# A 2-block transformer kernel on one Trainium2 core: narrow projections with their weight columns stationary, a reordered pool layer, and an output product that runs with tokens on the partitions

## The reference

```
# first block, mixer: proj = xn @ w_in; its last 80 columns are k_idx (64) and w_idx (16)
logits = einsum('bthd,bsd->bths', q_idx, k_idx)
idx_score = einsum('bth,bths->bts', w_idx * (IDX_HEADS**-0.5 * IDX_DIM**-0.5), relu(logits))
# pool layer: u, zu (1536 each), qm, zm (512 each) = split(rmsnorm(x) @ w_in)
y_pool = (windowed means of u, minus u) @ w_pool * scale * silu(zu)
y_mem = memory_attention(qm / sqrt(128), mem) * silu(zm)
x = x + concat([y_pool, y_mem]) @ w_out
# NSA layer: q (1536), gl (36), zq (1536), qm, zm (512 each) = split(rmsnorm(x) @ w_in)
gates = sigmoid(gl)                  # 12 heads x 3 branches
x = x + concat([nsa(q, gates, ...) * silu(zq), y_mem * silu(zm)]) @ w_out
return rmsnorm(x, final_g)
```

## Time and profile before

| | |
|---|---|
| median of 3 runs | 2564.04 us |
| profiled execution, its own time | 2564.2 us |
| its span, first to last instruction | 2562.5 us |
| mean granted TensorE clock | 0.965 |
| PE, PE weight load, POOL, ACT, DVE busy | 94%, 88%, 80%, 41%, 37% |

### The profile page before, as it was taken

The page is one execution under the profiler, slowest core; times in us unless marked ns, Lnnn a source line. Parts: engine busy times, 40 slices in busy tenths (PEclk is TensorE's granted clock), DMA queues, the critical chain, the costliest instruction groups (busy, mean ns, idle before and its releaser), DMA issues. The chain is left out here.

```text
span 2562.5 us, 43002 instructions
## 1 busy us (share of the span) xinstructions
PE 2406.2 (94%) x17211; PEld 2267.3 (88%) x17211; DVE 951.0 (37%) x1451; ACT 1044.7 (41%) x1308; POOL 2060.7 (80%) x1940
## 2 busy tenths in 40 slices
PE   6999999989998899999999999998899998999896
PEld 6989998768997798898998999998899888988896
DVE  5025662554152442031121131704516652255522
ACT  3344444554345333333333333434334333345532
POOL 6988994766786599999999998799787986865583
PEclk9999998999998899999999999999899998999998
DMA  5654433353443355655555555455354564533341
GB/s 183 197 165 148 147 121 120 116 197 116 165 148 116 115 166 196 196 174 194 191 180 197 182 180 177 156 184 161 120 181 148 165 191 153 163 107 116 100 164 50
DMA packets 206428, 400.17 MB, mean 156 GB/s; under 512 B 10434, under 2 KB 20932, under 8 KB 205252
## 3 DMA queue, kind: packets, MB, share of 16 engines
q1 hardware_dynamic: 206276, 397.99, 47.9%
HBM read 395.87 MB, written 2.10 MB: 155 GB/s over the span
## 5 line engine op out<-in xcount | busy, mean ns | idle before, releaser
L566 POOL TENSOR_TENSOR w_low<-ring,w_high 128x512 fp32r<-128x512 f32 (+3 forms) x1872 | 2050.9, 1128 | 457.7 <-ACT w_high L1091 450.1
L1091 ACT ACTIVATE w_high<-ring 128x1024 fp32r<-128x1024 f32 (+2 forms) x760 | 786.6, 1039 | 1364.0 <-PE bank L599 1351.3
L599 PE MATMUL bank<-x_high,w_high 128*128 128x256 f32 x4196 | 1220.3, 291 | 77.6 <-issue 32.6
L599 PE MATMUL bank<-x_low,w_high 128*128 128x256 f32 x4196 | 1203.8, 287 | 0.0
L599 PE MATMUL bank<-x_high,w_low 128*128 128x256 f32 x4196 | 1203.3, 287 | 0.0
L599 PEld LDWEIGHTS bank<-x_high,w_high 128*128 128x128 f32 x4196 | 822.7, 196 | 94.0 <-issue 50.0
L599 PEld LDWEIGHTS bank<-x_low,w_high 128*128 128x128 f32 x4196 | 823.0, 196 | 2.2 <-issue 2.0
L599 PEld LDWEIGHTS bank<-x_high,w_low 128*128 128x128 f32 x4196 | 822.1, 196 | 0.0
L599 PE MATMUL bank<-w_high,hidden 128*128 128x512 f32 x768 | 236.5, 389 | 0.0
L599 PEld LDWEIGHTS bank<-w_high,hidden 128*128 128x128 f32 x768 | 144.0, 188 | 29.7
L599 PE MATMUL bank<-w_high,x_high 128*128 128x512 f32 (+2 forms) x352 | 142.5, 405 | 9.0 <-DVE proj L1581 5.9
(11 more groups left out here) (272 smaller groups left out, 1961.5 us busy)
## 6 DMA issues: line engine op xcount, KB each, us to landing
ring<-in_w_in SPq DMA_DIRECT2D x64, 1024.0 KB, 5.4
ring<-in_w_up SPq DMA_DIRECT2D x64, 1024.0 KB, 5.2
ring<-in_w_down SPq DMA_DIRECT2D x64, 1024.0 KB, 5.1
ring<-in_w_out SPq DMA_DIRECT2D x48, 1024.0 KB, 5.1
ring<-in_a_w_in SPq DMA_DIRECT2D x32, 1024.0 KB, 5.3
ring<-in_b_w_in SPq DMA_DIRECT2D x32, 1024.0 KB, 5.3
ring<-in_w_kv SPq DMA_DIRECT2D x24, 1024.0 KB, 5.1
ring<-in_w_mem_kv SPq DMA_DIRECT2D x16, 1024.0 KB, 5.0
```

Source lines behind the costliest of these rows:

```text
L566: last = pool.tensor_tensor(w_low[:, u % UNITS, part], ring[:, u // 2, first:first + n], w_high[:, u % UNITS, part], ALU.subtract)
L599: mm = pe.matmul(out, lhs, rhs, start=start and n == 0, stop=stop and n == 2, skip_group_check=True)
L1091: act.activation(w_high[:, u % UNITS, 0:n], ring[:, u // 2, r0 * g.width:r0 * g.width + n], ACT.Copy)\
```

## The change

It has five parts. (a) `idx_tail` and `nsa_gate` use a new `narrow_unit`: the 80 or 36 weight columns are stationary and the 256 tokens move, 6 matmuls a unit in place of 12. The index keys then come out with features on the partitions and go straight to `ikT`; the 16 index weights and the 36 gates are turned by two transposes each (`idx_turned`, `turn_gates`). (b) The pool layer runs `pool_qm`, `pool_zm`, `pool_in`; the first 16 units of `pool_in` run beside the 4 memory heads, the windowed means are computed while later blocks of `pool_in` run, and `out0` takes its operand's last quarter first (`GATED_FIRST`). (c) ACT rounds 9 units in place of 6 before it waits for `turn_hidden`. (d) `out1` runs in `tokens_unit`; the residual `hT` is turned into `tokens` by 8 groups of 4 transposes between the units of `nsa_q` (`turn_h`), with a copy by ACT each. (e) The last norm runs on the token rows, block by block: DVE adds, multiplies by the gain (loaded as a broadcast of 1 MB), ACT squares with accumulation, then one root a row, a scaling shared by DVE and ACT, and a store in four pieces.

```diff
-     ("pool_in", 6, 6), ("pool_qm", 1, 1), ("pool_zm", 1, 1), ("pool_mix", 1, 4, 3, 384), ("out0", 4, 4),
+     ("pool_qm", 1, 1), ("pool_zm", 1, 1), ("pool_in", 6, 6), ("pool_mix", 1, 4, 3, 384), ("out0", 4, 4),
...
+        GATED_FIRST = (3, 0, 1, 2)
+        BESIDE_MEM0 = units_of("pool_in")[:16]
...
+        H_TURN_AFTER = (11, 13, 14, 16, 18, 20, 21, 22)
...
-        TOKENS_FIRST = ("attn_v", "cross_v", "mem_v0", "mem_v1", "nsa_gate")
+        TOKENS_FIRST = ("attn_v", "cross_v", "mem_v0", "mem_v1")
...
-        peel = g.blocks if g.blocks < 3 else int(g.b0 == 0)
+        peel = g.blocks if g.blocks < 3 or name == "out0" else int(g.b0 == 0)
...
+    out0_part = columns(w_out2[0:D, :], 0)
+    stream("out0", lambda n, j: out0_part(n, GATED_FIRST[j]))
...
+    sp.wait_ge(h_turned, 8)
+    sp.wait_ge(x_ready, x_made["nsa"] + 4)
+    sp.dma_start(final_gain, spread(a["final_g_2"].rearrange("(o n) -> o n", o=1), 0, P)).then_inc(final_gain_in, 16)
...
-    sp.wait_ge(final_kept, 8)
-    sp.dma_start(a["out"].rearrange("a (h p) n -> p (a h) n", p=P), tokens).then_inc(out_stored, 16)
...
+    out_rows = a["out"].rearrange("a (h p) n -> p (a h) n", p=P)
+    for piece in range(2):
+        for h in range(TH):
+            cols = slice(1024 * piece, 1024 * piece + 1024)
+            sp.wait_ge(final_rows[h], piece + 1)
+            sp.dma_start(out_rows[:, h, cols], tokens[:, h, cols]).then_inc(out_stored, 16)
+    sp.wait_ge(out_stored, 64)
...
+    def narrow_unit(g, b, u, pair, x, first, of):
+        pe.wait_ge(low_ready, 8 * b + u + 1)
+        wh, wl = parts(u, g)
+        r0, rows = g.unit(u)
+        for k in range(rows):
+            kt = first + r0 + k
+            mm = accumulate(pair[0][0:g.width, 0:T], (wh[:, k, :], wl[:, k, :]), x(kt),
+                            start=(kt == 0), stop=(kt == of - 1))
+        mm.then_inc(units_used, 1)
...
-            pe.wait_ge(idx_keys, 1)
+            pe.wait_ge(evacuated, PLAN["idx_tail"].g0 + 1)
             for h in range(TH):
-                mm = pe.transpose(bank[4][0:64, h * P:h * P + P], idx_rows[:, h, 0:64], ident[:, :])
+                mm = pe.transpose(bank[4][:, 16 * h:16 * h + 16], idx_w_rows[:, h * P:h * P + P],
+                                  ident[64:80, 64:80])
             mm.then_inc(idx_turned, 1)
         if n == 6:
-            pe.wait_ge(idx_keys, 2)
+            pe.wait_ge(idx_keys, 1)
+            pe.wait_ge(idx_weights, 1)
...
-    product("pool_in", features_unit, operand, made=x_made["pool"], sums=norm_sum)
-    product("pool_qm", features_unit, operand)
+    product("pool_qm", features_unit, operand, made=x_made["pool"], sums=norm_sum)
+    product("pool_zm", features_unit, operand)
     pe.wait_ge(evacuated, PLAN["pool_zm"].g0)
-    attend(MEM0, units_of("pool_zm"))
+    attend(MEM0, BESIDE_MEM0)
+    product("pool_in", features_unit, operand, begun=2)
...
+    product("out0", features_unit, lambda kt: operand(4 * GATED_FIRST[kt // 4] + kt % 4), made=x_made["pool_y"])
...
+        for h in range(TH):
+            mm = pe.transpose(bank[4][:, 36 * h:36 * h + 36], gate_rows[:, h * P:h * P + P], ident[0:36, 0:36])
+        mm.then_inc(gates_turned, 1)
...
+        pe.wait_ge(evacuated, PLAN["out0"].g0 + 4)
+        pe.wait_ge(silu_ready, 5)
+        if i:
+            pe.wait_ge(h_kept, i)
+        for k in range(4):
+            mm = pe.transpose(bank[4][:, k * P:k * P + P], hT[:, 4 * (i // 2) + k, (i % 2) * P:(i % 2) * P + P],
+                              ident[:, :])
+        mm.then_inc(h_turned, 1)
...
+    beside = {9: turn_hidden, 10: turn_gates, 12: second_layer, 15: swap_compressed}
...
+        if n in H_TURN_AFTER:
+            turn_h(H_TURN_AFTER.index(n))
...
-    product("out1", features_unit, operand, made=x_made["nsa_y"])
-    norm_sum()
...
-        if n >= 2:
-            pe.wait_ge(final_kept, n - 1)
-        h, c = n % 2, n // 2
-        for k in range(4):
-            mm = pe.transpose(bank[5 + n % 2][:, k * P:k * P + P], proj[:, 4 * c + k, h * P:h * P + P],
-                              ident[:, :])
-        mm.then_inc(final_turned, 1)
+    product("out1", tokens_unit, operand, made=x_made["nsa_y"])
...
+    high_parts("pool_qm", root)
+    high_parts("pool_zm")
+    attend(MEM0, BESIDE_MEM0)
+    def silu_of(t, group):
+        act.wait_ge(evacuated, group + 1)
         act.activation(pair_tile(t, 4), pair_tile(t, 4), ACT.Silu).then_inc(silu_ready, 1)
-    high_parts("pool_qm")
-    attend(MEM0, units_of("pool_zm"))
-    act.wait_ge(evacuated, PLAN["pool_mix"].g0)
-    act.activation(pair_tile(28, 4), pair_tile(28, 4), ACT.Silu).then_inc(silu_ready, 1)
+    silu_of(28, PLAN["pool_zm"].g0)
+    high(20)
+    silu_of(12, PLAN["pool_in"].g0 + 3)
+    high(8)
+    silu_of(16, PLAN["pool_in"].g0 + 4)
+    high(4)
+    silu_of(20, PLAN["pool_in"].g0 + 5)
...
-    high(6)
+    high(9)
...
+    high(1)
+    act.wait_ge(gates_turned, 1)
+    act.activation(nsa_gates[:, :, :].rearrange("p h n -> p (h n)"), bank[4][:, 0:36 * TH], ACT.Sigmoid)\
+       .then_inc(silu_ready, 1)
+    done = 14
+    for i, n in enumerate(H_TURN_AFTER):
+        high(n + 5 - done)
+        done = n + 5
+        act.wait_ge(h_turned, i + 1)
+        act.activation(tokens[:, i % 2, (i // 2) * 512:(i // 2) * 512 + 512], bank[4][:, :], ACT.Copy)\
+           .then_inc(h_kept, 1)
+    high(36 - done)
...
+    for j in range(4):
+        high(8)
+        act.wait_ge(evacuated, PLAN["out1"].g0 + j + 1)
...
+            act.activation(final_spare, tokens[:, h, 512 * j:512 * j + 512], ACT.Square,
+                           accum_out=final_sums[:, h, j:j + 1]).then_inc(final_squares, 1)
+    act.wait_ge(final_squares, 4 * TH)
+    act.activation(final_spare[:, 0:1], eps_col[:, 0:1], ACT.Sqrt)
+    act.wait_ge(final_summed, 1)
+    act.activation(final_dev, final_mean, ACT.Sqrt, scale=1.0 / D, bias=eps_col[:, 0:1]).then_inc(final_sqrt, 1)
+    act.wait_ge(final_root, 1)
+    act.activation(tokens[:, 1, 0:1024], tokens[:, 1, 0:1024], ACT.Copy, scale=final_scale[:, 1:2])\
+       .then_inc(final_rows[1], 1)
+    act.activation(tokens[:, 1, 1024:1536], tokens[:, 1, 1024:1536], ACT.Copy, scale=final_scale[:, 1:2])
+    act.activation(tokens[:, 1, 1536:D], final_last[:, 1, :], ACT.Copy, scale=final_scale[:, 1:2])\
+       .then_inc(final_rows[1], 1)
...
-    pair = bank[2 * (g.g0 % 2)], bank[2 * (g.g0 % 2) + 1]
-    for h in range(TH):
-        last = dve.tensor_scalar(idx_rows[:, h, 0:64], pair[h][:, 0:64], scale_col(h), None, ALU.mult)
...
+    tail = bank[2 * (g.g0 % 2)]
+    then(dve.tensor_tensor(ikT[0:64, :], tail[0:64, 0:T], scale_rows_[0:64, :], ALU.mult))
+    dve.tensor_copy(ikT[64:128, :], ikT[0:64, :]).then_inc(idx_keys, 1)
+    dve.scalar_tensor_tensor(out=idx_w_rows, in0=tail[64:80, 0:T], scalar=IDX_SCALE, in1=scale_rows_[64:80, :],
+                             op0=ALU.mult, op1=ALU.mult).then_inc(evacuated, 1)
...
-            dve.tensor_copy(ikT[64:128, :], bank[4][0:64, 0:T]).then_inc(idx_keys, 1)
+            dve.tensor_copy(idx_w[:, :, :].rearrange("p h n -> p (h n)"), bank[4][:, 0:16 * TH])\
+               .then_inc(idx_weights, 1)
+            dve.wait_ge(idx_weights, 1)
...
+    keep("pool_qm", scaled_tiles(24))
+    keep("pool_zm", scaled_tiles(28))
+    attend(MEM0, BESIDE_MEM0, {"pool_in": scaled_tiles(0)})
...
+    def pool_block(b):
+        read_out(PLAN["pool_in"], b, 0, scaled_tiles(0))
+        dve.wait_ge(evacuated, PLAN["pool_in"].g0 + b + 1)
+    pool_block(2)
+    dve.wait_ge(silu_ready, 1)
+    then(dve.tensor_tensor(pair_tile(24, 4), pair_tile(24, 4), pair_tile(28, 4), ALU.mult))
+    window(3)
+    pool_block(3)
+    window(2)
+    window(0)
+    pool_block(4)
+    window(1)
+    for n in range(4):
+        dve.wait_ge(units_used, behind("pool_in")((3 * n + 2) // 2))
+        split(pair_tile(32 + 3 * n, 3), flat(x_high, 3 * n, 3), flat(x_low, 3 * n, 3)).then_inc(x_ready, 1)
+    pool_block(5)
+    split(pair_tile(24, 4), flat(x_high, 12, 4), flat(x_low, 12, 4)).then_inc(x_ready, 1)
+    def pooled_y(c):
+        split(pair_tile(12 + 4 * c, 4), flat(x_high, 4 * c, 4), flat(x_low, 4 * c, 4)).then_inc(x_ready, 1)
     for j in range(4):
         g = PLAN["pool_mix"].g0 + j
+        dve.wait_ge(silu_ready, 2 + (3 * j + 2) // 4)
...
-    split_tiles("pool_y", (12, 16, 20))
-    split_gated("pool_y", 3, ((24, 28, 4),))
-    residual_and_operand("out0", 1, G_KV, behind("out0"))
+        dve.wait_ge(evacuated, g + 1)
+        if j:
+            pooled_y(j - 1)
+    residual_and_operand("out0", 1, G_KV, lambda u: behind("out0")((u + 2) % 8))
...
-        last = dve.tensor_scalar(nsa_gates[:, h, :], bank[2 * (g.g0 % 2) + h][:, 0:36], scale_col(h), None,
-                                 ALU.mult)
-    last.then_inc(evacuated, 1)
+    dve.tensor_tensor(gate_rows, bank[2 * (g.g0 % 2)][0:36, 0:T], scale_rows_[0:36, :], ALU.mult)\
+       .then_inc(evacuated, 1)
...
-    residual("out1")
-    fold()
-    scale_known()
-    for kt in range(KT):
```

(47 more changed lines are left out.)

61 lines of the change are left out of this document (27 added, 34 removed).

## The result

The changed kernel takes **2510.09 us**, the median of 4 runs (2508.24 to 2510.66); the kernel before, timed beside it, 2564.84 (2562.95 to 2569.09). The ratio is 0.978, with a 95% interval of 0.977 to 0.980. The prediction was 2489.4 with a range of 2481 to 2502: the direction was right, the time lies 8 us above the range, and of the 74.6 us forecast 54.8 came. The profiled execution took 2508.24 with a span of 2506.5.

What follows compares the result with a forecast made beforehand. PE, busy 94% of the span, was taken to bound the kernel. Savings of 12.3 + 22.5 + 12.9 + 5.1 + 21.8 = 74.6 us took the median from 2564.04 to 2489.4 us, range 2481 to 2502.

Steps and rivals of the forecast that it cites:

- (a) Index tail: Index tail and HGRN root chain behind it: 48 wide-moving matmuls replace 96, 12.3 us saved in all.
- the root chain's start: Behind the index tail: the chain of HGRN roots that paces the next stage starts 11.8 us earlier.
- (b) Pool layer: Pool layer through `cmp_kv`: waits and half clock of 24.7 us go, 0.9 and 1.3 come back, sum -22.5.
- The 9.04: Pool layer: PE's wait of 9.04 us for DVE, expected to go as `pool_qm` and `pool_in` run earlier.
- So nearly all 24.7 goes: Pool layer: nearly all 24.7 us of PE's waits and half clock vanish, with DVE's means beside `pool_in` blocks.
- what is late next: `pool_mix`: DVE's read-out, split and group 0 just meet PE's need; 0.9 us charged (0 to 4).
- `cmp_kv`: Fifth unit's wait for POOL grows from 2.8 to 4.1 us, as later residuals delay ACT's rounding; +1.3.
- Gate and `nsa_q`, -12.9: Gate and `nsa_q`: narrow gate, a new 1.8 us wait, no ACT stall or half-clock restart, added transposes; 12.9 us saved.
- `out1` and the end: `out1` falls to 89.2 us (-5.1); behind the last matmul 11.8 us remain (-21.8), with the store taken as 6.0.
- The clock in the narrow stretches: Rival: clock falls in narrow tail and gate too; costs 9 us, 2498; chance 0.14.
- DVE and POOL get in each other's way: Rival: contention at MEM0, `pool_mix` and `out1`; 4 us in `out1`, 3 to 4 in `pool_mix`, 2497; chance 0.13.
- The late load: Hidden-gain rival: a load late at `nsa_q`, or another start of the root chain; 5 to 12 us, 2498; chance 0.09.

Runs made afterwards that it cites:

- experiment 1: On the kernel before, only `idx_tail` moved to `narrow_unit`; 2558.65 us, ratio 0.9974.
- experiment 2: On the kernel after, the HGRN product kept in its PSUM bank instead of SBUF; 2505.69 us.
- experiment 12: On the kernel after, POOL's work on `attn_v` in two pieces of 512 columns a unit instead of four of 256; 2505.53 us.
- experiment 3: On the kernel after, the second memory's load issued between the second and third chunk of `wv_x` instead of ahead of all four; 2503.98 us.
- experiment 4: On the kernel before, the second memory's load issued between the second and third chunk of `wv_x`; 2564.21 us, ratio 0.9998.
- experiment 6: On the kernel after, DVE's windowed means left out, so `y_pool` isn't computed; 2500.93 us.
- experiment 11: On the kernel after, ACT rounds 6 units instead of 9 before waiting for the turned hidden rows; 2518.04 us.

## Why the prediction was wrong

- **(a) Index tail.** The tail (5.8 forecast; 402.90 to the first unit of `attn_v` takes 8.0 with the wait for POOL, 21.2 before) and the root chain's start (11.8, measured 11.9) were right. The step that failed is that the chain keeps this gain: -12.3 was forecast, -7.0 came. A start 11.9 earlier puts its first DVE product into POOL's unbroken row of `attn_v` pieces. It lasts 4.2 longer (experiments 1, 2 and 12), which is 2.8 at the unit of `attn_v` behind it, and up to 5.5 where the lower clock lasts longer as well. In the kernel after the stage so ends 1.1 short of the forecast. A further 2.5 is the load of experiments 3 and 4: it was a cost of 1.9 in the kernel before and is 4.5 in the one after. Why it grew wasn't isolated; the chunk's rounding ended ACT's wait at 515.66, 11.24 behind the issue, where before the last stretch of that wait was put down to PE (525.55, 10.29 behind it). The last 1.6 is the unit of `cross_v` at the lower clock, behind a wait that the kernel before has too; neither edit takes it away. Whether it comes with the change or by chance stays open.
- **(b) Pool layer.** The 9.04 and the two waits at `pool_mix` and `out0` went, as said. The failed step is "So nearly all 24.7 goes" with 0.9 for what is late next: the old waits went and new ones came in their place. I counted DVE's 34 us as hidden because PE had units to do beside them, and didn't ask what POOL makes of them, though the earlier trace rows show DVE slow beside POOL. POOL has 0.3 us to spare in a unit; beside DVE it is 0.5 behind. POOL finished a unit 4.9 us before PE began it, and this lead hid the deficit for a time: the means begin at 1746.5, the first wait comes at 1777.75. Waits of 9.8 were measured where 0.9 was charged. Without the means the layer is 7.2 shorter (experiment 6); the waits at `pool_zm` and `out0` stay without them.
- **`cmp_kv`.** +2.5 for 1.3. The wait in front of its fifth unit rose by 1.7, from 2.9 to 4.6, by the mechanism given: the last residual is added 9.9 behind the start of `cmp_kv` instead of 8.2. Not forecast was the lower clock behind it (0.57 from 1944 to 1948, 1.00 behind the shorter wait before), about 1.5; 0.7 at the sixth unit went.
- **Gate and `nsa_q`, -12.9**: right, with its pieces: the narrow gate, the new wait of 1.78, and the stall that part (c) takes away, which comes back without it (experiment 11).
- **`out1` and the end**: right within 0.5 and 0.8. POOL stayed ahead in `out1`. At the end the table load took 1.28 and ACT's next instruction followed 0.02 behind it; the store took 6.9 from its first issue instead of 6.0, which is nearly all that the end is longer by. In three of the other runs one of DVE's multiplications by the gain was held up there too, for 7.0 to 12.4 us, at no measurable cost.
- **Attention of the NSA layer, +1.6**: not forecast. 1.4 of it is one unit, the first of `nsa_zm`, before and after:

```profile
2388.29:2395.82 7.53, 6.27 (x46) 5.32 (x46) 4.46 (x18) 3.48 (x11) 2.83 (x4) 1.00 0.38 124
```
```profile
2357.48:2366.44 8.96, 7.70 (x45) 6.62 (x46) 4.46 (x18) 3.48 (x11) 2.82 (x4) 0.81 0.46 148
```

  PE's wait in this unit is 1.26 in both; the granted clock behind it is lower in the one after. Of the ten later traces of kernels built on after, three show the shorter value at clock 1.00 (experiments 2, 3 and 12) and seven 8.9 to 9.1, so it doesn't follow from the code of this stage.
- **The rivals.** The clock in the narrow stretches: refuted, 1.00 in both. The one that came is "DVE and POOL get in each other's way" (0.13, 2497), with its place too narrow: it named MEM0, `pool_mix` and `out1`, and it came at the means and the HGRN heads. The late load (0.09) came as well, with the weights of `cross_v` instead of those of `nsa_q`. The range left out the sum of two rivals, and two are what happened; even their sum, 2506, would have been too low.

## What to carry to other kernels

When a stage is made to start earlier, list what the engines that share a resource do in the new time window; DVE work moved beside a POOL that has 10% to spare isn't hidden when PE has units to do. Look for single instructions that last many times their shortest: the kernel before had one of 15 us in its trace, off the path. SP issues its loads in the order of the program, so one that waits for its buffer holds up the later ones, those with a free place too: moving one load behind two chunks was worth 6.1 us here.

## What the runs showed of the hardware

In these traces a DVE instruction with all its inputs and its output in SBUF was in some places kept out until POOL paused: 4.90 us instead of 0.69, 13.74 instead of 0.55, 15.10 instead of 2.00 at its shortest. This row and POOL's beside it stand in the trace of the kernel before, in the MLP, and were not read for the prediction:

```profile
937.62 15.10 DVE L1870 TENSOR_TENSOR heads_scratch<-heads_scratch 128x1024 f32<-128x1024 f32 x1
```
```profile
935.30 16.34 POOL L566 TENSOR_TENSOR w_low<-ring,w_high 128x512 fp32r<-128x512 f32 x13
```

It ends 1.08 us behind POOL's last piece (951.64), the 128x512 product 0.55 behind, the cast of 768 columns 0.41 behind. It happened with pieces of 256 and of 512 columns, and with one input (the cast) as with two. In the seven profiled runs with the narrow tail, four pieces a unit and the HGRN product in SBUF it came each time, 4.86 to 4.90 us. Yet elsewhere both take turns: beside POOL DVE's multiplications and subtractions of 768 columns in the means last 1.93 us (0.96 at their shortest) and POOL's pieces 1.70 instead of 1.29. What decides between taking turns and being kept out isn't settled by these runs.

The Trainium skill (SBUF — State Buffer, Who interferes with whom) names the instructions that contend with GpSimd: those with two SBUF inputs, and copies and casts in their two-port modes; not one with a single SBUF input outside these. Which instructions were held up here, the cast among them, and the free one of experiment 2 (0.69 us) agree with it. It lets the loser wait for the other's instruction; a wait through eleven of POOL's pieces, as in the MLP, is more than it says.
